# First block's up products: unnormalised operand, root applied at read-out, four pairs of banks, one convolution tap added on GpSimd

## What is computed

```python
h = h + rmsnorm(mix, g[1])
ff = conv_ffn(rmsnorm(h, g[2]), ffn_w_up[l], ffn_conv[l], ffn_w_down[l])

def conv_ffn(x, w_up, conv_w, w_down):
    u = causal_dwconv(x @ w_up, conv_w)
    gate, val = jnp.split(u, 2, axis=-1)
    return (jax.nn.silu(gate) * val) @ w_down
```

## Time and profile before

| | us |
|---|---|
| runs of the kernel | 1577.25, 1578.69, 1581.88 (median 1578.69) |
| the profiled execution: its own time | 1577.86 |
| the profiled execution: span of its instructions | 1576.1 |
| TensorE busy | 1458.9 (93% of the span) |
| VectorE busy | 1042.8 (66%) |
| ScalarE busy | 780.3 (50%) |
| GpSimd busy | 282.8 (18%) |

### The profile page before, as it was taken

One profiled execution on the slowest core, in us unless ns is written; L12 is line 12 of the kernel. 1 busy time (PEld: TensorE's weight loads), 2 busy tenths in 40 slices (PEclk: granted clock), 3 DMA queues, 4 the chain that ended last, 5 costly groups with the idle time before them and its releaser, 6 DMA issues. The chain is left out here.

```text
span 1576.1 us, 29025 instructions
## 1 busy us (share of the span) xinstructions
PE 1458.9 (93%) x11301; PEld 1397.5 (89%) x11301; DVE 1042.8 (66%) x1727; ACT 780.3 (50%) x1272; POOL 282.8 (18%) x384
## 2 busy tenths in 40 slices
PE   5999879999787997999988899989999988999997
PEld 4999769999787876999987789989999987899997
DVE  5664678877775546788877755357877675587643
ACT  5654644544355544555535555565343554544341
POOL 0000102220054420122001143102332100122210
PEclk9999999999998998999998999999999998999999
DMA  7432525659522213565872311136775733275451
GB/s 279 177 128 107 189 98 221 225 172 346 204 107 107 81 55 107 193 237 208 323 280 73 116 54 55 64 124 222 280 254 207 240 113 134 107 277 211 146 177 45
DMA packets 41140, 265.80 MB, mean 169 GB/s; under 512 B 4560, under 2 KB 5712, under 8 KB 15440
## 3 DMA queue, kind: packets, MB, share of 16 engines
q1 hardware_dynamic: 41040, 264.44, 46.6%
HBM read 263.38 MB, written 1.05 MB: 168 GB/s over the span
## 5 line engine op out<-in xcount | busy, mean ns | idle before, releaser
L224 DVE TENSOR_TENSOR w_lo<-raw,w_hi 128x2048 fp32r<-128x2048 f32 (+2 forms) x207 | 426.3, 2064 | 215.0 <-ACT w_hi L220 211.2
L220 ACT ACTIVATE w_hi<-raw 128x2048 fp32r<-128x2048 f32 (+3 forms) x224 | 385.9, 1727 | 37.8 <-PE bank L414 33.7
L412 PE MATMUL bank<-x_hi_up,w_hi 128*128 128x272 f32 (+1 forms) x704 | 203.7, 289 | 8.3 <-DVE x_lo_up L717 8.1
L414 PE MATMUL bank<-x_hi_up,w_lo 128*128 128x272 f32 (+1 forms) x704 | 201.8, 287 | 0.0
L413 PE MATMUL bank<-x_lo_up,w_hi 128*128 128x272 f32 (+1 forms) x704 | 201.4, 286 | 0.0
L412 PE MATMUL bank<-z_hi,w_hi 128*128 128x258 f32 x704 | 200.5, 285 | 0.0
L413 PE MATMUL bank<-z_lo,w_hi 128*128 128x258 f32 x704 | 198.9, 283 | 0.0
L414 PE MATMUL bank<-z_hi,w_lo 128*128 128x258 f32 x704 | 198.2, 282 | 0.0
L412 PEld LDWEIGHTS bank<-x_hi_up,w_hi 128*128 128x128 f32 x704 | 133.4, 190 | 10.3 <-issue 8.8
L413 PEld LDWEIGHTS bank<-x_lo_up,w_hi 128*128 128x128 f32 x704 | 133.9, 190 | 0.0
L413 PEld LDWEIGHTS bank<-z_lo,w_hi 128*128 128x128 f32 x704 | 133.4, 190 | 0.1
(11 more groups left out here) (461 smaller groups left out, 3888.0 us busy)
## 6 DMA issues: line engine op xcount, KB each, us to landing
raw<-w_up SPq DMA_DIRECT2D x44, 1024.0 KB, 4.8
raw<-w_gu SPq DMA_DIRECT2D x44, 1024.0 KB, 4.8
work<-w_ada SPq DMA_DIRECT2D x27, 1024.0 KB, 5.1
raw<-w_down SPq DMA_DIRECT2D x32, 704.0 KB, 5.6
raw<-w_dn SPq DMA_DIRECT2D x32, 704.0 KB, 4.1
raw<-w_a_in SPq DMA_DIRECT2D x16, 1024.0 KB, 5.5
mod_w_down<-w_ada SPq DMA_DIRECT2D x16, 1024.0 KB, 6.0
raw<-w_gdn_qkv SPq DMA_DIRECT2D x12, 1024.0 KB, 4.8
```

Of the source, the lines that this page charges most:

```text
L220: act.activation(w_hi[:, s, 0:blocks * P], raw[:, s, 0:blocks * P], ACT.Copy).then_inc(hi_split.sem, 1)
L224: dve.tensor_tensor(w_lo[:, s, 0:blocks * P], raw[:, s, 0:blocks * P], w_hi[:, s, 0:blocks * P].bitcast(F32), ALU.subtract).then_inc(lo_sp ...
L412: pe.matmul(o, w_hi[:, s, b], x_hi[:, xk, cols[0]:cols[1]], start=begin, stop=False)
L414: last = pe.matmul(o, w_lo[:, s, b], x_hi[:, xk, cols[0]:cols[1]], start=False, stop=end)
```

## The change

Both up products (up0 and up1) and their down products are built in another way:

- **Entry.** `BranchEntry` takes the place of `NormEntry`. For each tile k: weight the branch, add it to h, and at once x_hi = h * gain on ScalarE, x_lo = h * gain - x_hi on VectorE. The operand lacks the second root. Squares are made by ScalarE behind each high part, gathered by two wide VectorE adds, and summed with two matmul calls by ones.
- **First two items.** `first_two` interleaves items 0 and 1 over the k tiles, item 1 two tiles behind, in four banks; the root's matmuls come after both.
- **Banks.** Four pairs of banks in turn (`groups=4`), so item r needs item r - 4 read out, where before it needed item r - 2. The down products use banks 4 and 5.
- **Read-out.** VectorE makes z = bank * root (two instructions); the banks are free after that. ScalarE makes tap 2 into `conv` and tap 1 into `tap1`, both from z (four instructions, before two). GpSimd adds tap 1 to `conv` (two new instructions ahead of its split). VectorE adds tap 0 from z (two instructions, before four with PSUM), then the product.
- **Order.** ScalarE: high part of item r + 3, taps of r, silu of r. VectorE: z of r, low part of r + 3, modulation column, tap 0 of r, product of r.
- **Loads.** The first load of a modulation column waits for the sum of squares, before for the last x_lo.

```diff
+                    def first_two():
+                        lag = 2
+                        pe.wait_ge(lo_split.sem, first + 1)
+                        for m in range(k_tiles + lag):
+                            ...
+                            for i, kk in ((0, m), (1, m - lag)):
+                                ...
+                        root.pe_root(pe)
...
-                        early = not act_late or isinstance(r, int) and r == first + n - 1
+                        early = paired or not act_late or isinstance(r, int) and r == first + n - 1
...
+                        if groups == 4 and not halves:
+                            pe.wait_ge(item_out.sem, first + 1 if isinstance(i, int) and i == first + 3 else i - 3)
...
+            def dve_out(dve, j, s, where):
+                item_ready(dve, up, j)
+                if not isinstance(j, int) or j >= 1:
+                    dve.wait_ge(tapped.sem, tapped.at(j * 4))
+                    dve.wait_ge(conved.sem, conved.at(j * 2))
+                for t in range(2):
+                    dve.tensor_tensor(z[:, t, :], where(t)[:, 0:width_in], rstd[:, c0:c1], ALU.mult).then_inc(z_made.sem, 1)
+                dve.wait_ge(z_made.sem, z_made.at(j * 2 + 2))
+                dve.sem_inc(item_out.sem, 1)
...
             def act_out(act, j, s, where):
+                for t in range(2):
+                    act.wait_ge(z_made.sem, z_made.at(j * 2 + (t + 1)))
+                    ...
+                    act.activation(conv[:, s % 2, t, :], z[:, t, lead:width_in], ACT.Copy,
+                                   scale=weight(j, 2, t)).then_inc(tapped.sem, 1)
+                    act.activation(tap1[:, t, skip(1):width], z[:, t, lead + skip(1) - 1:width_in - 1], ACT.Copy,
+                                   scale=weight(j, 1, t)).then_inc(tapped.sem, 1)
+
+            def dve_conv(dve, j, s, where):
+                for t in range(2):
+                    dve.wait_ge(added.sem, added.at(j * 2 + (t + 1)))
+                    d = conv[:, s % 2, t, skip(2):width]
+                    dve.scalar_tensor_tensor(d, z[:, t, lead + skip(2) - 2:width_in - 2], weight(j, 0, t), d, ALU.mult,
+                                             ALU.add).then_inc(conved.sem, 1)
...
             def pool_out(pool, j, s):
+                for t in range(2):
+                    pool.wait_ge(tapped.sem, tapped.at(j * 4 + (2 * t + 2)))
+                    d = conv[:, s % 2, t, skip(1):width]
+                    pool.tensor_tensor(d, d, tap1[:, t, skip(1):width], ALU.add).then_inc(added.sem, 1)
                 pool.wait_ge(multiplied.sem, multiplied.at(j + 1))
```

More of the change, by code:

```diff
@@ L249, in __init__ @@
                          sqrt_next=False, room=None, room_free=None, room_ready=None, squares=None, x_ready=None, x_step=1, x_pair=1, x_off=0,
[L250 removed]
+                         resid=None, root=None, work_free=None, before=None, between=None, opened=0, paired=False, groups=2):
                 first, n, blocks = starts[name]
@@ L254, in where @@
                 def where(r, s, t):
+                    if halves and groups == 4:
+                        return bank[4 + ((s - first) % SLOTS) // 2]
                     if halves:
                         return bank[4 * (first % 2) + ((s - first) % SLOTS) // 2]
+                    if groups == 4:
+                        return bank[2 * ((s - first) % SLOTS) + t]
                     return bank[4 * ((s + (1 if opened else 0)) % 2) + t]
@@ L342, in step @@
                     def step(r, s, turn):
-                        early = not act_late or isinstance(r, int) and r == first + n - 1
+                        early = not act_late or isinstance(r, int) and (r == first + n - 1 or paired and r == first)
                         if resid and isinstance(r, int) and r == first + n - 1:
@@ L384, in both_tiles @@
                         return last
+                    def first_two():
+                        lag = 2
+                        pe.wait_ge(lo_split.sem, first + 1)
+                        for m in range(k_tiles + lag):
+                            if m == lag:
+                                pe.wait_ge(lo_split.sem, first + 2)
+                            if m < k_tiles:
+                                pe.wait_ge(entry.split.sem, entry.split.at(m + 1))
+                            for i, kk in ((0, m), (1, m - lag)):
+                                if not 0 <= kk < k_tiles:
+                                    continue
+                                s = (first + i) % SLOTS
+                                for t in range(tiles):
+                                    o = where(first + i, s, t)[:, 0:width]
+                                    b = slice((t * k_tiles + kk) * P, (t * k_tiles + kk + 1) * P)
+                                    pe.matmul(o, w_hi[:, s, b], x_hi[:, kk, cols[0]:cols[1]], start=kk == 0, stop=False)
+                                    pe.matmul(o, w_hi[:, s, b], x_lo[:, kk, cols[0]:cols[1]], start=False, stop=False)
+                                    last = pe.matmul(o, w_lo[:, s, b], x_hi[:, kk, cols[0]:cols[1]], start=False,
+                                                     stop=kk == k_tiles - 1)
+                                if kk == k_tiles - 1:
+                                    last.then_inc(item_done.sem, 1)
+                        root.pe_root(pe)
                     def step(r, s, turn):
                         i = r
+                        if paired and isinstance(r, int) and r <= first + 1:
+                            if r == first:
+                                first_two()
+                            return
                         pe.wait_ge(lo_split.sem, i + 1)
-                        if not halves:
+                        if groups == 4 and not halves:
+                            pe.wait_ge(item_out.sem, first + 1 if isinstance(i, int) and i == first + 3 else i - 3)
+                        elif not halves:
                             if not isinstance(i, int) or i >= 2:
@@ L887, in dve_out @@
[L887 to L902, removed]
@@ L904, in act_late, with weight @@
-            def act_late(act, j, s, where):
[L905 to L910, removed]
+            skip = lambda back: max(0, back - lead)
+            def weight(j, tap, t):
+                return par("conv", j + ((layer * 3 + tap) * 2 + t) * FF_TILES)
@@ L928, in pool_out @@
                 pool.tensor_tensor(lo, prod[:, s % 2, :], hi.bitcast(F32), ALU.subtract).then_inc(halved.sem, 1)
[L930 to L940, removed]
+            return Product(up, 2, KD, x_hi, x_lo, cols, act_out=act_out, dve_out=dve_out, pool_out=pool_out,
+                           act_late=act_late, dve_late=dve_late, entry=entry, root=entry, paired=True, groups=4,
+                           room=one_room, room_ready=(entry.summed, 1),
+                           signals=(("z_made", 2 * n), ("tapped", 4 * n), ("taps_added", 2 * n), ("conved", 2 * n),
+                                    ("silued", n), ("multiplied", n), ("a_high", n), ("a_split", n)))
         def gated_product(name, x_hi, x_lo, a_hi, a_lo, phase, root, room_free):
@@ L2801, in fused_model @@
                 run(fox, b_out)
-        ffn_layer(1, late, gain1(1, 2), "up1", "down1", (gain1(1, 1), True), 1)
+        ffn_layer(1, late, gain1(1, 2), "up1", "down1", gain1(1, 1))
         modulation_scales(((0, 1, "norm_mix"), (0, 4, "norm_ffn"), (1, 1, "norm_mix")))
```

113 lines of the change are left out of this document (86 added, 27 removed).

## The result

| | median us | runs |
|---|---|---|
| kernel before | 1579.72 | 1577.25 to 1581.88 |
| changed kernel | 1623.29 | 1619.78 to 1624.64 |

The ratio is 1.0274, with a 95% interval of 1.0253 to 1.0294: **43.6 us slower**, where the prediction had 22.3 slower and a range that ended at 1617. The profiled execution took 1622.23 us, span 1620.4.

What follows compares the result with a forecast made beforehand. TensorE, never idle in steady up, was taken to bound the kernel; the new serial chain would outlast it. Entry gains, turns, columns and ends netted +9.0 us in up0, +13.3 in up1: 1601.0 us, range 1576 to 1617.

Steps and rivals of the forecast that it cites:

- The entry: Start of each up product: first matmul at 203.5 instead of 213.11, item 2 9.5 us earlier in up0, 9.2 in up1.
- The direction and the chain: Steady up items: silu, high part, low part, first addition, tap 0 in series, 5.75 us before holds; kernel slower, +22.3 us.
- Rival 1: Steady up items: GpSimd's additions run beside VectorE's low part, kernel faster, 1565 us; chance 0.20.
- rival 2: Steady up items: only the low part holds GpSimd, turns 5.75 and 5.65, 1590 us or 1583; chance 0.21.
- Rival 3: Steady up items: VectorE always gets in first, turns 6.5 and 6.4, 1622 us; chance 0.10.
- I take 0.25: Steady turn: 0.25 us added for short GpSimd and VectorE instructions holding each other, giving 6.0 us in up0, 5.9 in up1.
- 2.78, of which I take 2.65: Six items per up product: the modulation column before tap 0 adds a mean 2.65 us each, 15.9 in all.
- the last three turns 3.5 off: End of each up product: halves of 1408 columns shorten the high and low parts, 3.5 us less in all.
- its split takes 1.3: End of up0: after the last product at 363.4, its split takes 1.3 us, ahead of the last matmuls' 0.4.
- The rule on the port: VectorE instructions with two SBUF inputs and GpSimd's SBUF reads exclude each other; taken whole, turn 6.5, 1622 us.

Runs made afterwards that it cites:

- run 2: Changed kernel with GpSimd's additions of tap 1 left out, so tap 1 is missing from the result: 1567.44 us, ratio to before 0.9954.
- run 7: Changed kernel with only GpSimd's second addition left out, so the value half misses tap 1: 1604.47 us, ratio to before 1.0158.
- Run 5: Changed kernel with silu and product one item behind, taps 1 and 0 on VectorE from PSUM, GpSimd only splitting: 1571.51 us, ratio to before 0.9961.
- run 6: Kernel of Run 5 with the last modulation column of each up product after the last two products: 1562.81 us, ratio to before 0.9893.
- run 8: Kernel of run 6 with VectorE's last column waiting until GpSimd has split the last product: 1565.78 us, ratio to before 0.9927.
- run 4: Changed kernel with ScalarE's taps ahead of the high part of the item three on, as before the change: 1680.67 us.

## Why the prediction was right or wrong

The forecast of 1601.0 us failed in the price of one turn: the holds between GpSimd and VectorE were taken at 0.25 us a turn and measure 0.53 (6.28 less 5.75), the column and the last turns were priced without them, and TensorE's lower clock behind the last wait was not in the sum.

**The entry: right.** In up0 its marks hold within 0.3 us once the shift of 0.76 is off, TensorE's third item starts 9.5 us earlier as predicted, and run 2 shows the new entry paying once the chain is short. In up1 the product of item 0 comes 26.1 us behind the first root, where 25.5 was predicted.

**The direction and the chain: right.** The turn has the predicted links in the predicted order, the first addition ends 0.62 after the low part as predicted (run 7), TensorE waits for `w_lo` at hosted items by up to 2.9 us, and for the split at the second down item. Without the additions the turn is 5.02 where the steps give 5.75 - 0.62 = 5.13. Rival 1 (additions beside the low part) is excluded by their 1488 ns; rival 2 (5.75) by 6.25. Rival 3 gave nearly the measured time, 1622, but by luck: it had VectorE always in first, with turns of 6.5; in the trace GpSimd goes in first, in front of taps and column halves, and the non-hosted turns are 6.25. The hosted turns and the end bring the rest.

**Three terms of the sum were mis-sized.** For up0, by silus from 225.22 to 371.26, 146.04 us against a predicted 126.0 + 15.9 - 3.5 = 138.4:

- *"I take 0.25"* for the mutual holds of short instructions. Bounds of 0 to 0.75 were right, the value was not: 13 turns without a column take 81.7 us, so 6.28 each, +3.7. The rows I took it from showed a VectorE instruction lengthened by 0.19 and 0.31. What the changed kernel and runs 7 and 2 show behind it: an addition that already waits goes in as soon as VectorE's instruction ends, and holds the next for 0.49 to 0.57 us of its 0.78. Run 5 has an exception, the subtraction that lets one column half go ahead of it; what decides the order there stays open.
- *"2.78, of which I take 2.65"* for a column. That priced the column at its old duration. With two held halves of 1.78 it has to pay the same hold twice, three of the first five hosted turns are 9.06 instead of 8.65 and two 8.64: +1.2, and +1.2 for the last one, which also stands among the short turns.
- *"the last three turns 3.5 off"*: two are 5.6, not 4.83, since their low parts of 1.62 are held to 2.15 by the subtraction: +1.5.

Together 7.6 us; up1 by the same count 143.55 against 136.3, 7.25.

**One term was missing, one short.** The sum led to the last split tile and took TensorE's work behind it at full clock. After an idle stretch of 8 us the granted clock is 0.50, with 19 matmuls at 0.235 instead of 0.125, and 2.1 us are lost before it is back. That was in reach: the earlier trace rows shows 0.52 after the idle stretch of the entry. And "its split takes 1.3" left out the last product's own length: from its start at 371.72 to the end of its split at 373.48 it is 1.76 us, 1.69 in up1.

The account of up0: 185.69 us between the marks (before 166.54), so +19.15 = 9.0 predicted + 7.6 turns + 0.45 last split + 2.1 clock. In up1 +22.85 = 13.3 + 7.25 + 0.6 product of item 0 + 0.4 last split + 1.3, what is left for the clock. The remaining 2.3 of the span's 44.3 us lie outside both, 0.76 of it ahead of the first root.

**The rule on the port.** The held cast beside halves of a column in run 6 (1.41 us, and 0.41 in run 8 with VectorE idle) bears out, but for an overlap of some 0.15 us, what the Trainium skill says on the page "SBUF — State Buffer", section "Who interferes with whom": whoever is first has the port pair for the whole instruction. I had that rule beside the sum and gave its full effect a tenth. The turn, 6.28, lies half way between the forecast's 6.0 and the 6.5 of the full effect.

## What to carry to other kernels

Where GpSimd and VectorE work in one loop, add up GpSimd's time and that of VectorE's instructions with two SBUF operands as for a single engine, and compare the sum with the turn: here some 2.8 us and 4.2 us (a share of the column included) against TensorE's 6; the mean turn in up0 became 6.95. Then ask where a step waits on both: it is the serial path through the engines' lists (run 4), and putting silu and product one item behind, with taps read from PSUM and no additions on GpSimd, took the ratio to the kernel before from 1.027 to 0.996, and a later last column to 0.989. No run separates the three parts of that edit. When a sum ends in a long wait of TensorE, add the matmuls at the lower clock behind it, here 2.1 us behind a wait of 8.02.

## What I had not expected of the hardware

- A GpSimd addition of 0.78 us slips in between two VectorE instructions that stand back to back, the two halves of a column: 1.22 us became 1.78.
- Two GpSimd instructions took 3.03 us beside halves of a column (1.62 + 1.41) and 1.18 us (0.77 + 0.41) with VectorE idle.
- The same program had 57 matmuls in 8 us of one execution and 30 in the same 8 us of another, TensorE at work in both, the granted clock 1.00 and 0.57. It cost 3.3 us.
